# Attention turned onto key partitions: row maxima from a first rounded pass, no turning of probabilities, row sums from ones beside the values

## What is computed

```python
q = (rms_norm(cq) @ w_uq)        # 8 heads x (64 + 32 rotary)
kv = (rms_norm(ckv) @ w_ukv)     # 8 heads x (64 key + 64 value); k_rope is shared
s = q_nope . k_nope + q_rope . k_rope          # 1024 x 1024 for each head
p = softmax(s * 96 ** -0.5);  y_at = p @ v
y = concat(rms_norm(y_hyena), rms_norm(y_lru), rms_norm(y_at))   # 256 + 256 + 512
x = layer_norm(alpha * x + y @ w_out)          # "mix"
x = layer_norm(alpha * x + expert_choice_moe(x))
```

## Time and profile before

| | |
|---|---|
| median of 3 runs | 1734.79 us (1734.51 to 1738.61) |
| the profiled execution's own time | 1728.14 us |
| its span | 1726.3 us |
| mean granted TensorE clock | 0.964 of 2.4 GHz |
| busy: PE, DVE, ACT, POOL | 92%, 61%, 44%, 14% |

### The profile page before, as it was taken

The page is one execution under the profiler, slowest core; times in us unless marked ns, Lnnn a source line. Parts: engine busy times, 40 slices in busy tenths (PEclk is TensorE's granted clock), DMA queues, the critical chain, the costliest instruction groups (busy, mean ns, idle before and its releaser), DMA issues.

```text
span 1726.3 us, 18249 instructions
## 1 busy us (share of the span) xinstructions
PE 1593.0 (92%) x6870; PEld 1144.6 (66%) x6870; DVE 1060.0 (61%) x1250; ACT 757.9 (44%) x854; POOL 244.4 (14%) x139
## 2 busy tenths in 40 slices
PE   5999989999989998999999898179999999999997
PEld 2444467854334345998988787158888888888874
DVE  6312234351442336667776454759999899989886
ACT  5201100023240212445554233147777777777773
POOL 0400000000000000000000332401332233223304
PEclk9999999999999999999999899579999999999998
DMA  5606000071100000000000333949999999999995
GB/s 186 217 0 225 25 1 1 0 136 28 49 1 0 0 0 25 1 1 26 25 25 1 136 121 108 368 171 361 378 378 371 379 379 379 370 378 379 379 370 217
DMA packets 152864, 284.58 MB, mean 165 GB/s; under 512 B 25268, under 2 KB 35842, under 8 KB 152803
## 3 DMA queue, kind: packets, MB, share of 16 engines
q1 hardware_dynamic: 147187, 263.28, 42.9%
q0 software_dynamic: 4464, 16.25, 3.6%
q10 hardware_dynamic: 1152, 4.19, 0.6%
HBM read 259.07 MB, written 24.64 MB: 164 GB/s over the span
## 4 chain that ended last, share of the span: by engine, by line
PE 81%; DVE 8%; ACT 4%; DMA 4%; issue 2%; POOL 0%; POOLq 0%; ACTq 0%; SPq 0%; DVEq 0%
PE psum L944 15%; PE psum L1247 9%; PE psum L1249 9%; PE psum L1248 9%; PE psum L1134 5%; PE psum L1085 4%; PE psum L928 3%; PE psum L979 3%; DMA arena<-in_exp_w_down 3%; PE psum L1124 3%; PE psum L1193 2%; PE psum L1195 2%; PE psum L1194 2%; PE psum L989 2%; PE psum L990 2%
## 5 line engine op out<-in xcount | busy, mean ns | idle before, releaser
L1682 DVE TENSOR_TENSOR split_at<-arena,split_at 128x2048 fp32r<-128x2048 f32 x188 | 427.8, 2290 | 60.5 <-ACT split_at L823 59.1
L823 ACT ACTIVATE split_at<-arena 128x2048 fp32r<-128x2048 f32 x192 | 367.3, 1915 | 63.4 <-PE psum L1249 53.4
L1247 PE MATMUL psum<-split_at,split_at 128*128 128x512 f32 x768 | 305.9, 398 | 1.4 <-DVE split_at L1688 1.4
L1249 PE MATMUL psum<-split_at,split_at 128*128 128x512 f32 x768 | 300.3, 391 | 0.0
L1248 PE MATMUL psum<-split_at,split_at 128*128 128x512 f32 x768 | 299.6, 390 | 0.0
L944 PE MATMUL psum<-arena 128*128 128x512 f32 (+1 forms) x608 | 265.9, 596 | 3.7 <-DVE arena L1358 3.7
L944 PEld LDWEIGHTS psum<-arena 128*128 128x128 f32 (+1 forms) x608 | 113.5, 188 | 151.7 <-issue 147.1
L1249 PEld LDWEIGHTS psum<-split_at,split_at 128*128 128x128 f32 x768 | 144.5, 188 | 31.2
L1247 PEld LDWEIGHTS psum<-split_at,split_at 128*128 128x128 f32 x768 | 144.8, 189 | 29.8 <-DVE split_at L1688 1.8
L1248 PEld LDWEIGHTS psum<-split_at,split_at 128*128 128x128 f32 x768 | 144.9, 189 | 28.3
L758 ACT ACTIVATE arena<-psum,arena 128x1024 f32<-128x1024 f32 x64 | 71.2, 1113 | 130.1 <-DVE arena L1555 130.1
(11 more groups left out here) (265 smaller groups left out, 2200.6 us busy)
## 6 DMA issues: line engine op xcount, KB each, us to landing
arena<-in_exp_w_gate SPq DMA_DIRECT2D x64, 1024.0 KB, 14.2
arena<-in_exp_w_up SPq DMA_DIRECT2D x64, 1024.0 KB, 14.1
arena<-in_exp_w_down SPq DMA_DIRECT2D x64, 1024.0 KB, 14.2
arena<-in_w_in SPq DMA_DIRECT2D x9, 1024.0 KB, 5.3
arena<-in_x SPq DMA_DIRECT2D x8, 512.0 KB, 4.4
xhat_scratch<-arena SPq DMA_DIRECT2D x8, 512.0 KB, 6.2
arena<-in_w_out SPq DMA_DIRECT2D x8, 512.0 KB, 3.2
arena<-xhat_scratch SPq DMA_DIRECT2D x8, 512.0 KB, 4.9
```

The lines of the kernel that those rows point to most:

```text
L823: a(flat(wsplit[c % WS][0]), wraw[:, c], ACT.Copy).then_inc(s_whi, 1)
L1247: mm(bank(out_bank), src[0][:, k, :], whi[:, k % 4, :], start=(k == 0), stop=False)
L1249: ins = mm(bank(out_bank), src[1][:, k, :], whi[:, k % 4, :], start=False, stop=(k == KT - 1))
L1682: tt(flat(lo), wraw[:, c], flat(hi), ALU.subtract).then_inc(s_wlo, 1)
```

## The change

Scores are now made with the keys on the partitions, so the exponential's result is already in the form that `pv` needs, and nothing is turned. The maximum over keys can then not be a bias. So each head has a first pass, `rough`: high by high only, queries on the partitions, 2 matmuls for each 128 queries; DVE reduces it to the negated maximum `nm`. `max_turn` turns these into a row of 1024, ACT writes that row as a 97th contraction row of the high queries (`max_row`), and the high keys have a row of ones there (`key_ones`). For head 0 the rough pass lies in the heads stage, for head h+1 inside head h's units. The scale goes into the copies of the queries.

`pv` has 64 value columns and 64 columns of ones as its stationary operand and 512 probabilities as the moving one, 4 instructions a unit, in banks 6 and 7 over the whole head. ACT copies them out once a head (`o_copy`), DVE divides in four parts (`o_scale`). head_low from head 1 on, and the low parts of w_out and of the groups, move from DVE to POOL.

The heads' output stays turned. Its norm is no longer applied ahead of the projection: the projection is in two halves of 24 matmuls, the first for the other two groups (banks 0/1), the second for the heads (banks 2/3), and DVE adds the second times the norm's factor. The squares are summed by TensorE with a column of ones (4 float32 matmuls a block). The high and low parts of the heads' output are made block by block, on ACT and POOL, inside the mix stage.

The diff's core (short lines are joined here, so that it fits):

```diff
+ROUGH_AFTER = {U_HEAD0 + 1: (0, 1), U_HEAD0 + 3: (3, 4), U_HEAD0 + 4: (7,)}
+ROUGH_WITHIN = {(U_HEAD0 + 4, 1): 5, (U_HEAD0 + 4, 3): 6}
+MAX_FIRST = {0: 0, 1: 1, 2: 2, 3: 3, 4: 4, 5: 6}
+MAX_SECOND = {4: 5, 5: 7}
+ROWS_AT = {4: 0, 6: 1}
 # TensorE, heads stage
+def rough_first(qt):
+    if qt == 0: pe.wait_ge(s_qkh, 3)
+    if qt >= 2: pe.wait_ge(s_nm, qt - 1)
+    if qt == 3: pe.wait_ge(s_qro, 2)
+    rough(0, qt, 2 * (qt % 2))
 # TensorE, attention
+def rough_next(h, qt):
+    if qt == 0: pe.wait_ge(s_qkh, 2 * h + 4)
+    pe.wait_ge(s_nm, TT * h + qt)
+    if qt == 4: pe.wait_ge(s_mr, 2 * h + 1)
+    rough(h, qt, 4)
+def pv(n):
+    h, kb = divmod(n, TT)
+    pe.wait_ge(s_exp, n + 1)
+    if kb == 0:
+        pe.wait_ge(s_vs, h + 1)
+        if h: pe.wait_ge(s_ot, h)
+    for j in range(2):
+        ins = mm(bank(6 + j), v1[:, h % 2, kb, :], p_at[:, n % 2, HALF * j:HALF * j + HALF], start=(kb == 0), stop=(kb == TT - 1))
+max_turn(0, 0); max_turn(0, 1); scores(0)
+for n in range(N_UNIT):
+    h, kb = divmod(n, TT)
+    if n + 1 < N_UNIT: scores(n + 1)
+    if h + 1 < NH and kb in ROWS_AT: max_turn(h + 1, ROWS_AT[kb])
+    if h + 1 < NH and kb in MAX_FIRST: rough_next(h + 1, MAX_FIRST[kb])
+    pv(n)
+    if h + 1 < NH and kb in MAX_SECOND: rough_next(h + 1, MAX_SECOND[kb])
 # ACT, attention
+key_ones(1); rotary_high(1); head_high(1, 0); head_high(1, 1)
+max_row(0, 0); max_row(0, 1)
+probs(0)
+for n in range(NH * TT):
+    if h and qt == 0: o_copy(h - 1)
+    if n + 1 < N_UNIT: probs(n + 1)
+    if h + 1 < NH and qt in ROWS_AT: max_row(h + 1, ROWS_AT[qt])
+    if h + 2 < NH and qt == 7:
+        head_high(h + 2, 0)
+        head_high(h + 2, 1)
 # DVE, heads stage, u == 8, behind the LRU reciprocal
+for qt in ROUGH_AFTER.get(u, ()): row_max(0, qt, 2 * (qt % 2))
+if u == len(HEADS) - 2:
+    for qt in ROUGH_WITHIN.values(): row_max(0, qt, 2 * (qt % 2))
 # DVE, attention: 4 for each head
+def o_scale(p):
+    link(v.reciprocal(o_inv[:, p % 2, :], o_raw[DV:P, cols]))
+    tt(yT_at[DV * (h % 2):DV * (h % 2) + DV, h // 2, cols], o_raw[0:DV, cols], o_inv[:, p % 2, :], ALU.mult).then_inc(s_ov, 1)
 # POOL, mix stage
+def heads_out_low(i):
+    pool.wait_ge(s_oh, i + 1)
+    if i >= 2: pool.wait_ge(s_mix, i - 1)
+    pool.tensor_tensor(ya_lo[:, i % 2], yT_at[:, :, P * i:P * i + P], ya_hi32[:, i % 2], ALU.subtract).then_inc(s_ol, 1)
+heads_out_low(0); heads_out_low(1)
 for i in range(TT):
     pool.wait_ge(s_xh[i % 2], 16 * (i // 2 + 1))
     link(pool.tensor_tensor(res, res, gin, ALU.mult))
     pool.tensor_tensor(res, res, bin_, ALU.add).then_inc(s_res, 1)
+    if i + 2 < TT: heads_out_low(i + 2)
 # ACT, mix stage
+heads_out(0); heads_out(1)           # each: high part, then squares
 for i in range(TT + 2):
     if i < TT:
+        heads_root(i)
         act.wait_ge(s_x1, i + 1)
...
         a(accb[:, i % 2, :], x1t[:, i % 2, :], ACT.Copy, scale=ALPHA).then_inc(s_acc, 1)
...
     if 1 <= i <= TT:
         act.wait_ge(s_x1p, 2 * i - 1)
...
         a(x1T[(i - 1) % 2][:, 0:HALF], bank(4), ACT.Copy).then_inc(s_x1ta, 1)
+    if i + 2 < TT: heads_out(i + 2)
     if i >= 2: router_exp(i - 2)
 # DVE, mix stage
-v.wait_ge(s_mix, i + 1)
+v.wait_ge(s_mxa, i + 1)
 v.wait_ge(s_res, i + 1)
+stt(x, xres[:, b, :], ALPHA, bank(0, 2), ALU.mult, ALU.add).then_inc(s_mxau, 1)
+v.reciprocal(ars[:, i:i + 1], asd[:, i:i + 1]).then_inc(s_on, 1)
+v.wait_ge(s_mix, i + 1)
+stt(x, bank(2, 2), ars[:, i:i + 1], x, ALU.mult, ALU.add).then_inc(s_mixu, 1)
 # TensorE, mix stage, block i: first half waits for s_mxau >= i; sums of squares;
 # second half waits for s_ol >= i + 1 and s_mixu >= i; then x1_turn(i-1), logits(i-2)
```

More of the change, by code:

```diff
@@ L188, in encoder @@
         yT_hy = mem(50128, 2, T)
[L189 removed]
+        v_at = mem(9168, TT, NH * DV)
         rot = mem(784, 128)
@@ L732, in rotary_high, with probs, max_row, key_ones @@
                 a(ks[slot][0][DV:DQ, :], kr[DV:DQ, :], ACT.Copy).then_inc(s_qkh, 1)
-            def probs_copy(n):
-                act.wait_ge(s_tr, 2 * n + 1)
+            def probs(n):
+                act.wait_ge(s_qk, n + 1)
                 if n >= 2:
                     act.wait_ge(s_pv, n - 1)
-                a(pT[:, n % 2, 0:HALF], bank(4), ACT.Copy).then_inc(s_pta, 1)
+                a(p_at[:, n % 2, :], bank(2 * (n % 2), 2), ACT.Exp).then_inc(s_exp, 1)
+            def max_row(h, half):
+                act.wait_ge(s_tr, 2 * h + half + 1)
+                a(qs[h % 2][0][DQ:DQ + 1, HALF * half:HALF * half + HALF], bank(0 if h == 0 else 4)[0:1, :], ACT.Copy).then_inc(s_mr, 1)
+            def key_ones(slot):
+                a(ks[slot][0][DQ:DQ + 1, :].rearrange("p (a b) -> p a b", a=8), ones[DQ:DQ + 1, :].unsqueeze(1).to_broadcast([1, 8, 128]),
+                  ACT.Copy).then_inc(s_k1, 1)
+            def o_copy(h):
+                act.wait_ge(s_pv, TT * (h + 1))
+                if h:
+                    act.wait_ge(s_ov, 4 * h)
+                a(o_raw, bank(6, 2), ACT.Copy).then_inc(s_ot, 1)
             for u in range(len(HEADS)):
@@ L752, in _ @@
             act.wait_ge(s_qro, 2)
+            key_ones(1)
+            rotary_high(1)
+            head_high(1, 0)
+            head_high(1, 1)
+            for half in range(2):
+                max_row(0, half)
+            probs(0)
             for n in range(NH * TT):
                 h, qt = divmod(n, TT)
[L755 to L765, removed]
+                if h and qt == 0:
+                    o_copy(h - 1)
+                if n + 1 < N_UNIT:
+                    probs(n + 1)
+                if h + 1 < NH and qt in ROWS_AT:
+                    max_row(h + 1, ROWS_AT[qt])
+                if h + 2 < NH and qt == 7:
+                    head_high(h + 2, 0)
+                    head_high(h + 2, 1)
                 if n in WOUT_AT:
@@ L770, in _, with heads_out, heads_root @@
                 if n in GROUPS_AT:
-                    g, c = divmod(GROUPS_AT.index(n), 2)
-                    act.wait_ge(s_qkl, 2 * NH + 2)
+                    m = GROUPS_AT.index(n)
+                    g, c = divmod(m, 2)
+                    act.wait_ge(s_qkp, 6)
                     act.wait_ge(s_rb, 3)
[L774 to L790, removed]
+                    a(y_hi[g][:, c, :], (yT_hy, hs)[g][:, c, :], ACT.Copy).then_inc(s_yh, 1)
+            o_copy(NH - 1)
+            def heads_out(i):
+                act.wait_ge(s_ov, N_PAIR - TT // 2 + i // 2 + 1)
+                if i >= 2:
+                    act.wait_ge(s_mix, i - 1)
+                o = yT_at[:, :, P * i:P * i + P]
+                a(ya_hi[:, i % 2], o, ACT.Copy).then_inc(s_oh, 1)
+                a(o_sq[:, i % 2], o, ACT.Square).then_inc(s_sq, 1)
+            def heads_root(i):
+                act.wait_ge(s_ssq, SUMS + i + 1)
+                a(asd[:, i:i + 1], bank(7)[:, i:i + 1], ACT.Sqrt, scale=1.0 / (NH * DV), bias=eps).then_inc(s_rsd, 1)
+            heads_out(0)
+            heads_out(1)
             def router_exp(i):
@@ L1070, in _, with rough @@
             sum_squares(9, False, True)
+            def rough(h, qt, b):
+                q, k = qs[h % 2][0], ks[h % 2][0]
+                for j in range(2):
+                    ins = mm(bank(b + j), q[0:DQ, P * qt:P * qt + P], k[0:DQ, HALF * j:HALF * j + HALF], start=True, stop=True)
+                ins.then_inc(s_max, 1)
+            def rough_first(qt):
+                if qt == 0:
+                    pe.wait_ge(s_qkh, 3)
+                if qt >= 2:
+                    pe.wait_ge(s_nm, qt - 1)
+                if qt == 3:
+                    pe.wait_ge(s_qro, 2)
+                rough(0, qt, 2 * (qt % 2))
             for u, (kind, i) in enumerate(HEADS):
@@ L1179, in _, with mix @@
             pe.wait_ge(s_wol, KT)
-            y = [(group[0][:, c, :], group[1][:, c, :]) for group in (y_hy, y_lru, *y_at) for c in range(2)]
+            pe.wait_ge(s_yl, 4)
+            def mix(b0, k, high, low, first, last):
+                for j in range(2):
+                    out_, cols = bank(b0 + j), slice(HALF * j, HALF * j + HALF)
+                    mm(out_, high, wout[k][0][:, cols], start=first, stop=False)
+                    mm(out_, high, wout[k][1][:, cols], start=False, stop=False)
+                    ins = mm(out_, low, wout[k][0][:, cols], start=False, stop=last)
+                return ins
@@ new lines, in _ @@
+                    for k in range(4):
+                        ins = mix(0, k, y_hi[k // 2][:, k % 2, P * i:P * i + P], y_lo[k // 2][:, k % 2, P * i:P * i + P], k == 0, k == 3)
+                    ins.then_inc(s_mxa, 1)
+                    pe.wait_ge(s_sq, SUMS + i + 1)
+                    if i == 0:
+                        pe.wait_ge(s_ov, N_PAIR)
+                    else:
+                        pe.wait_ge(s_rsd, ROOTS + i)
+                    for c in range(4):
+                        ins = mm(bank(7)[:, i:i + 1], o_sq[:, i % 2, c, :], ones[:, 0:1], start=(c == 0), stop=(c == 3))
@@ L1196, in _ @@
+                    ins.then_inc(s_ssq, 1)
```

(34 more changed lines are left out.)

300 lines of the change are left out of this document (168 added, 132 removed).

## The result

The changed kernel takes 1744.31 us (median of 6 runs, 1742.01 to 1746.19), the one before 1735.4 (6 runs): a ratio of 1.0049, 95% interval 1.0036 to 1.0062. It is slower by 8.9 us, where 7.1 were forecast and 1741.9 predicted. The profiled execution's span is 1742.6 us.

The account below looks back on a forecast made before the run. TensorE's instruction stream was taken to bound attention and mix, with a ring over other engines in the new mix. Start +21.1, attention -27.7, mix +13.7 sum to +7.1 us: 1741.9 us, range 1727 to 1757 for 8 in 10.

Parts of the forecast that it names:

- The start: From the heads stage's start to the first score: rough passes, DVE's queue and ACT's chain make it 21.1 us longer.
- the gap at rough 5: In u=9 TensorE idles 7.4 us, as rough 5's maximum stands behind DVE's reciprocal; half of what follows runs slow, +2.
- Attention: First score to last pv: turns removed, rough passes and waits added, 249.9 us against 277.6, so -27.7.
- Wait (a): Attention, kb=4: rough 4 waits for ACT, which does probs(n+1) ahead of max_row; 1.4 us, 7 times, 9.8 in all.
- Wait (b): Each head's end: next head's pv waits for ACT's probs, two head_highs and o_copy; 0.8 us, 6 times, 4.8 in all.
- The mix stage: Last pv to last x1: 137.0 us against 123.3, so +13.7; at most +17, at least +1.6.
- The ring: Mix stage: ACT's copy and high part, POOL's low part and res, DVE's adds; 16.4 us from x1 to x1, up to x1(6).
- Block 7: Last mix block, with no low part ahead of its res: x1(7) comes 11.9 us behind x1(6).
- 1, that the ring doesn't bind: Rival: a mix block is TensorE's 14.4 us, the mix stage costs +1.6, total -5.0, 1729.8 us; chance 0.20.
- 4, that the start is cheaper: Rival: at the start rough 5 doesn't wait long, -9 us, so -2 in all, 1733 us; chance 0.07.
- 2, the clock: Rival: waits in attention and mix blocks drop TensorE's clock to 0.50, +22 us, 1764 us; chance 0.08.
- 3, the lock: Rival: POOL's lock delays o_scale products on DVE, hence the maxima, plus late low parts, +11 us, 1753 us; chance 0.15.

Follow-up runs that it names:

- e2_start: Changed kernel with the LRU reciprocal and its two products moved from u=8 to behind unit 5 of the attention: 1736.01 us.
- e6_rough_twice: Changed kernel with each rough pass of heads 1 to 7 computed twice into the same bank, 112 matmuls more: 1765.29 us.
- e3_row_first: Changed kernel with ACT doing max_row ahead of the exponential, probs(n+1), at kb=4: 1738.19 us.
- e4_act_start: Changed kernel with ACT doing both max_row of head 0 ahead of head 1's high parts at the attention's start: 1740.85 us.
- e1_ring: Changed kernel with POOL making heads_out_low(i+2) behind res(i+1), not ahead of it: 1729.0 us.
- e5_all: Changed kernel with four edits together (POOL's low part, LRU products, max_row, ACT's start), the LRU products now behind unit 13: 1712.04 us.

## Why the prediction was right

**The start, +21.1 forecast, +21.1 measured.** The gap at rough 5 was forecast at 7.4 us and is 7.19, released by DVE behind the reciprocal; from u=8's end to the first score 29.6 were forecast and 29.5 came. e2_start shows that the cause is DVE's order: without the reciprocal and the products ahead of the maxima the stretch is 8.9 shorter. That the sum is right to a tenth is luck: in e6_rough_twice, which has the same start, the slow clock behind the gap lasted longer, eight matmuls taking 6.23 us and not 4.70, and the stretch was 1.6 longer.

**Attention, -27.7 forecast, -25.6 measured.** Wait (a), 1.4 us seven times, is 1.37 and 9.6 in all. Wait (b) was forecast at 0.8 six times; TensorE waited about 0.3 for head_high and 0.3 for o_copy at each boundary, 3.5 in all. Two terms were summed too small. The unit is 3.58 us where 3.55 were summed, since a score matmul's distance to the next is 0.234 (five of them from 713.86 to 715.03) and not 0.229, about 2 us over the stage. That price could be read beforehand: in the earlier trace rows five score matmuls take from 843.53 to 844.70, which is 0.234 each. And pv(0) starts 6.0 us behind the first score (704.74), where 5.4 were summed: fourteen matmuls at clock 0.50, 0.43 each. Against the 1.3 us that wait (b) was put too high, that leaves about 1 of the 2.1 us by which the stage exceeded the forecast without a place. The 97th row costs nothing visible: L1263 (97 rows) and L1264 (96) are 0.23 or 0.24 from the next one's start alike. e6_rough_twice shows that the stage is TensorE's stream.

**The mix stage, +13.7 forecast, +14.9 measured.** The ring was summed to 16.4 and is 16.3 to 16.6, once 15.9, six of them 97.7 us where 98.4 were forecast; x1(0) was put at 26.6 behind the last pv and is at 26.9. One term was not foreseen: POOL's scaling of w_out takes 2.84 us, not 2.4, and its last low part held TensorE's first mix matmul for 1.0 us; x1(0) came no later for it, as it hangs on the last o_scale. Block 7 came 13.7 behind block 6 and not 11.9, as TensorE ran part of it at clock 0.50; in e3_row_first and e4_act_start, whose profiles have a clock of 1.00 there, it came 12.1 behind. These 1.6 us of clock are more than the 1.2 by which the stage exceeded the forecast. e1_ring shows the ring to be the cause of the rest. The forecast's 13.6 us a block for the kernel before holds only for its last three.

**The rivals.** 1, that the ring doesn't bind, and 4, that the start is cheaper, fall by the traces and by e1_ring and e2_start. 2, the clock, is wrong for the attention (0.99 over the stage). In the mix stage the clock did fall (0.93 over x1(0) to x1(7)), but up to x1(6) it cost nothing: with 0.50 behind 1036.4 the block took 16.3 us, and the next, at 1.00 throughout, 16.4. Only block 7, behind the ring, paid for it. 3, the lock, is there but small: the 32 products of o_scale have a median of 0.42 us and a longest of 1.91. That one lies at the end, where the forecast had put it, beside a POOL product:

```profile
957.34 2.34 POOL L580 TENSOR_TENSOR arena<-arena 128x1024 f32<-128x1024 f32 x1
958.05 1.91 DVE L1723 TENSOR_TENSOR arena<-arena 64x256 f32<-64x256 f32 x1
```

The product ends 0.3 us behind POOL's instruction (959.68). In e2_start two products grew from 2.36 to 6.02 us, and the second ended 1.1 us, about its own length, behind POOL's L540 (726.09). The Trainium skill (SBUF — State Buffer, Who interferes with whom) states an exclusive lock for such a pair, a DVE instruction with two SBUF inputs and a GpSimd instruction that reads SBUF. The trace agrees in both places.

Open: why the stretch ahead of the heads stage varies by up to 6 us between executions the runs don't show, and e4_act_start's share of e5_all's gain rests on one trace.

## What to carry to other kernels

When work is moved from the busiest engine, sum up the others' queues in order as well. Here one stage became 25.6 us shorter, and most of that was given back by two such places: a reciprocal that stood ahead of a maximum (9 us), and a low part that stood ahead of a residual and closed a ring over three engines, ACT, POOL and DVE (12 to 14 us). A ring is found by following one result around until it comes back one iteration later. If its sum is longer than the busiest engine's work of an iteration, it sets the pace, and a swap of two instructions on an engine that is mostly idle (POOL, busy 20%) can open it. Here the order of each queue and the rows of the kernel before were enough to forecast three stretches with errors of 0.0, 2.1 and 1.2 us. What they did not give is the clock, which moved a stretch by 1.6 us from one execution to the next.

## What the runs showed of the hardware that was not expected

A gap in TensorE's work can be followed by a slow clock in one execution and not in another, though it is equally long and stands at the same place of the same code. In the mix stage TensorE waits for the first add of each block. Ahead of x1(1) the gap is 3.08 us, first in the changed kernel and then in e4_act_start, whose edit lies elsewhere; each line of a gap is followed by that of the 6 us behind it:

```profile
984.19:987.27 3.08, 0.00 (x1) 0.00 (x0) 1.27 (x2) 0.00 (x0) 1.70 (x1) 1.00 0.00 0
987.27:993.27 6.00, 6.00 (x19) 4.79 (x20) 5.41 (x8) 0.29 (x1) 0.00 (x0) 0.72 0.00 0
983.50:986.58 3.08, 0.00 (x1) 0.00 (x1) 1.27 (x2) 0.00 (x0) 1.70 (x1) 1.00 0.00 0
986.58:992.58 6.00, 6.00 (x29) 4.99 (x29) 5.41 (x8) 0.29 (x1) 0.00 (x0) 1.00 0.00 0
```

Ahead of x1(3) the gap is half as long, and the changed kernel keeps its clock while e3_row_first loses it:

```profile
1018.31:1019.82 1.51, 0.00 (x1) 0.00 (x1) 1.28 (x2) 0.00 (x0) 0.14 (x1) 1.00 0.00 0
1019.82:1025.82 6.00, 6.00 (x29) 5.06 (x30) 5.05 (x8) 0.30 (x1) 0.00 (x0) 1.00 0.02 4
1014.75:1016.29 1.54, 0.00 (x0) 0.00 (x1) 1.28 (x2) 0.00 (x0) 0.17 (x1) 0.76 0.00 0
1016.29:1022.29 6.00, 6.00 (x14) 4.80 (x15) 5.05 (x8) 0.30 (x1) 0.00 (x0) 0.50 0.00 1
```

The columns are as in the earlier trace rows: length, busy time of each engine, the clock, DMA. So the length of the gap does not settle it. What does, the runs don't show.
